# Router logits computed inside the output projection loop, expert ranks from two products, first gathers ahead of the eleventh expert's weights

## The chip, the cores and the metric

The kernel runs on one core of one Trainium2 chip. The metric is the device time of one execution in microseconds (us), as the median of several runs. Beside it stands one profiled execution, from which every duration here is taken. PE is the matrix engine; DVE, ACT and POOL are the vector, scalar and GpSimd engines, SP the engine that issues most DMAs.

## What is computed

One inference step of a decoder layer for 512 prompt rows and 8 sample rows of width 1024: a mixer (a recurrent half and a windowed attention half), cross attention to 256 memory rows, and a mixture of experts. The change touches only the way from the cross attention's output projection into the experts:

```python
x = x + memory_cross_attention(rms_norm(x, lp['norm_cross']), mem_k, mem_v, lp)   # ends in o @ lp['w_co']
x = x + hierarchical_moe(rms_norm(x, lp['norm_ffn']), lp)

def hierarchical_moe(h, lp):
    lg = (hf @ lp['w_group_router'] + lp['b_group_router']).astype(F32)      # 4 groups
    gsel = jnp.argmax(lg, axis=-1)
    p_sel = jnp.sum(jax.nn.softmax(lg, axis=-1) * onehot_g, axis=-1)
    le = (hf @ lp['w_expert_router'] + lp['b_expert_router']).astype(F32)    # 4 groups x 8 experts
    top_v, top_i = lax.top_k(le_sel, TOP_K)                                  # two experts of the chosen group
    top_w = jax.nn.softmax(top_v, axis=-1)
    ...
    # each expert: silu(h @ w_gate) * (h @ w_up) * weight, then @ w_down; summed over the row's two experts
```

## The kernel before, in words

The program is written engine by engine, each engine's instructions in a fixed order, joined by semaphores. Rows are held in five tiles: four of 128 prompt rows (t = 0 to 3) and one of the 8 sample rows (t = 4, `TILES`). PE writes into eight PSUM banks in the order of one list (`bank_plan`, L111): the n-th entry uses bank n mod 8, and PE waits until the entry eight places earlier has been emptied by DVE ("v") or ACT ("a").

The cross attention ends in the loop over `WC_ORDER` = csT, 0, cpT, 1, co, 2, coT, 3, 4. The numbers are the output projections of the row tiles (`cross_output`, L1411, PE); the names are the sample rows' attention: scores transposed (csT), weights transposed (cpT), values (co), outputs transposed (coT). After the projection of tile t, PE transposes the normalised rows of tile t − 1 (`xT3`). On DVE, `residual` (L2122) adds the two halves of the projection to x, empties and scales the transposed rows of the tile before (`gained`, L2145), waits for ACT's sum of squares and its root, and scales the row (L2143); ACT then writes the normalised rows to DRAM (`hn_d`), from where they are gathered later.

After the loop the routing follows, all of it in one chain between PE and DVE:

- PE multiplies all five tiles by the router weights, 36 columns (4 groups and 32 experts), eight products of depth 128 a tile. A float32 product appears as two instructions in the trace.
- DVE adds the bias (L2205), finds the group (`first_max`, L2211), sends the group exponents to ACT and waits for them (L2222 to L2225), masks the other groups, finds the two best experts, and writes a 0/1 table `Mk` of 32 experts for each tile (L2238).
- PE turns the table into ranks, that is, how many rows before this one chose the same expert: for each tile one product with a matrix of ones that goes to all later tiles and the total, and one with a triangular matrix (the loop before `slots`). Meanwhile DVE computes the weights of the two experts (L2240 to L2244).
- DVE turns ranks into slots in blocks of 64 rows (L2246 to L2274) and builds two tables for the ten columns (five tiles, two choices): which block and which row in it (L2275 to L2279). PE multiplies these and so gets for each slot the number of its row. While PE does so, DVE computes which expert an overflow block belongs to (L2281 to L2286, signal `s_eid`).
- DVE makes row indices of it (L2289 to L2297, signal `s_idx`), POOL starts three gathers of 128 normalised rows each (two blocks of 64, L824), and PE starts the 32 expert blocks: transposes (L1473), gate and up products (L1487), down products (L1501).

Expert weights, three loads of 512 KB per expert, go through eleven places in SBUF (`load_expert`, L705). SP issues the first ten while the cross attention and the routing run, each where the place comes free; the tenth waits until the router products have been emptied (its place holds the router weights), the eleventh for `s_idx` (its place holds the routing tables). From the twelfth on each waits for the down products of the block whose place it takes. The router weights themselves (four small loads, L695 to L699) are issued behind the last loads of the cross attention; only PE waits for them, before its router products.

## Time and profile before

| | us |
|---|---|
| median of 3 runs | 850.98 |
| lowest and highest run | 844.87, 852.36 |
| the profiled execution | 848.17 |
| its span, first to last instruction | 846.0 |
| PE busy in the span | 707.3 (84%) |
| DVE busy | 368.9 (44%) |
| mean granted clock of PE | 0.889 of full speed |

The profile comes from one execution. A busy time says how long an engine worked, not that the end waited for it; that is told by the chain, which goes back from the last instruction through whatever released each step. Loads on PE's weight side (PEld) run beside its products. The granted clock is a share of full speed: 1.00 is 2.4 GHz, 0.50 is 1.2 GHz.

### The profile page before, as it was taken

The numbers are of one execution on the slowest core, as the hardware profiler recorded it, in microseconds if no ns is written. First come the engines' busy times: TensorE is split into PE (matmuls) and PEld (weight loads), VectorE is DVE, ScalarE is ACT, GpSimd is POOL, SyncE is SP. The second block draws the span as 40 slices with busy tenths as digits, with TensorE's granted clock in tenths as the row PEclk, the third lists the DMA queues.
The fourth block names the chain that finished last, engine by engine and source line by source line (L and its number), as shares of the span: only waits on it lengthen the run. The fifth ranks groups of instructions, "written<-read, shape, count | busy, mean of one in ns | idle before, by whom it ended". The sixth has DMA issues, their size and how long they took to land.

```text
span 846.0 us, 16080 instructions
## 1 busy us (share of the span) xinstructions
PE 707.3 (84%) x6972; PEld 537.5 (64%) x6972; DVE 368.9 (44%) x717; ACT 214.9 (25%) x538; POOL 92.3 (11%) x122
## 2 busy tenths in 40 slices
PE   4999999999879889567979989858798249999943
PEld 3874887878878878556844458645347247777721
DVE  4210139992365674645682230463143632222217
ACT  4250114334222212434501011331121002222214
POOL 0100000000864000000000000000000013443210
PEclk9999999999999999859989989975896559999966
DMA  9622240002101000410507020032539448999826
GB/s 316 232 100 99 100 148 1 1 1 58 60 3 54 4 3 4 138 22 2 206 1 298 1 100 0 26 100 74 182 125 398 175 143 330 408 405 406 332 78 250
DMA packets 42491, 113.89 MB, mean 135 GB/s; under 512 B 10187, under 2 KB 12677, under 8 KB 41116
## 3 DMA queue, kind: packets, MB, share of 16 engines
q1 hardware_dynamic: 36964, 102.18, 32.7%
q0 software_dynamic: 4864, 8.53, 2.8%
q10 hardware_dynamic: 592, 2.13, 0.7%
q8 instruction: 56, 0.92, 0.4%
q14 instruction: 15, 0.12, 0.0%
HBM read 105.88 MB, written 16.24 MB: 144 GB/s over the span
## 4 chain that ended last, share of the span: by engine, by line
PE 72%; DVE 17%; ACT 4%; issue 3%; DMA 3%; SPq 0%; POOLq 0%; DVEq 0%
PE bank L868 52%; PE bank L1487 7%; PE bank L872 5%; PE bank L1501 4%; PE bank L1473 3%; DVE arena L1911 1%; PE bank L1495 1%; DMA arena<-in_norm_mix 1%; DMA arena<-pair_d 1%; DVE arena L2093 1%; DMA arena<-hn_d,arena 1%; DVE arena L2025 1%; DVE arena L2344 1%; DVE arena L2172 1%; ACT arena L1731 1%
## 5 line engine op out<-in xcount | busy, mean ns | idle before, releaser
L868 PE MATMUL bank<-arena 64*64 64x64 f32 (+12 forms) x5172 | 532.1, 297 | 61.8 <-DMA arena<-pair_d 11.4
L868 PEld LDWEIGHTS bank<-arena 64*64 64x64 f32 (+5 forms) x5172 | 399.0, 160 | 183.6 <-issue 94.2
L872 PE MATMUL bank<-arena 128*128 128x128 f32 (+4 forms) x392 | 57.5, 299 | 52.3 <-issue 16.7
L872 PEld LDWEIGHTS bank<-arena 128*128 128x128 f32 (+4 forms) x392 | 49.9, 166 | 67.5 <-issue 27.5
L1487 PEld LDWEIGHTS bank<-arena 128*64 128x64 f32 x1024 | 58.6, 138 | 19.8 <-issue 19.8
L824 POOL DMA_INDIRECT arena<-hn_d,arena x16 | 16.7, 1044 | 443.9 <-DVE arena L2297 420.1
L1487 PE MATMUL bank<-arena 128*64 128x128 f32 x1024 | 63.5, 277 | 0.0
L2304 DVE TENSOR_TENSOR arena<-bank,arena 128x512 f32<-128x512 f32 x32 | 22.1, 692 | 59.4 <-PE bank L1473 59.4
L1592 ACT COPY arena<-bank 128x260 f32<-128x260 f32 x40 | 15.0, 375 | 108.7 <-PE bank L868 108.7
L828 POOL DMA_INDIRECT pair_d<-arena x32 | 31.8, 993 | 61.1 <-ACT arena L1794 54.1
L2135 DVE TENSOR_TENSOR arena<-arena,bank 128x512 f32<-128x512 f32 x16 | 11.0, 687 | 61.4 <-PE bank L868 61.4
L1692 ACT COPY arena<-bank 128x256 f32<-128x256 f32 x56 | 20.8, 372 | 65.5 <-PE bank L868 64.4
L1501 PE MATMUL bank<-arena 128*64 128x512 f32 x128 | 35.4, 632 | 0.9 <-ACT arena L1790 0.9
L1731 ACT ACTIVATE arena<-arena 128x1024 f32<-128x1024 f32 (+1 forms) x10 | 10.6, 1057 | 97.4 <-DVE arena L2135 90.6
L1867 DVE COPY arena<-arena 128x9 f32<-128x9 f32 x14 | 2.4, 172 | 68.1 <-ACT arena L1592 67.9
L1473 PE MATMUL bank<-arena 128*128 128x128 f32 x128 | 23.4, 312 | 9.4 <-DMA arena<-hn_d,arena 9.4
L1794 ACT COPY arena<-bank 128x512 f32<-128x512 f32 x32 | 18.7, 585 | 46.2 <-PE bank L1501 46.2
L781 POOL TENSOR_TENSOR arena<-arena 128x256 f32<-128x256 f32 x8 | 5.0, 621 | 184.7 <-PE bank L868 184.7
L1473 PEld LDWEIGHTS bank<-arena 128*128 128x128 f32 x128 | 17.6, 197 | 11.5 <-issue 9.5
L2315 DVE TENSOR_TENSOR arena<-arena,bank 128x64 f32<-128x64 f32 x32 | 7.1, 221 | 40.6 <-ACT arena L1788 40.6
L2047 DVE TENSOR_TENSOR arena<-arena,bank 128x256 f32<-128x256 f32 x40 | 16.3, 420 | 12.3 <-PE bank L868 11.7
L2162 DVE TENSOR_REDUCE arena<-bank 128x2 f32<-128x512 f32 x8 | 5.5, 689 | 33.9 <-PE bank L868 33.8
(235 smaller groups left out, 545.8 us busy)
## 6 DMA issues: line engine op xcount, KB each, us to landing
arena<-in_w_exp_gate SPq DMA_DIRECT2D x32, 512.0 KB, 11.8
arena<-in_w_exp_up SPq DMA_DIRECT2D x32, 512.0 KB, 15.0
arena<-in_w_exp_down SPq DMA_DIRECT2D x32, 512.0 KB, 15.7
arena<-in_w_in SPq DMA_DIRECT2D x5, 2048.0 KB, 9.4
arena<-in_x_prompt SPq DMA_DIRECT2D x8, 512.0 KB, 6.1
arena<-in_w_out SPq DMA_DIRECT2D x2, 2048.0 KB, 11.0
arena<-in_cache_mem_k SPq DMA_DIRECT2D x8, 512.0 KB, 7.2
arena<-in_cache_mem_v SPq DMA_DIRECT2D x8, 512.0 KB, 3.8
```

The costliest lines, as they stand in the source:

```text
L824: pool.indirect_dma_start(dst, None, hn_d, bass.IndirectOffsetOnAxis(rows.bitcast(U32), 0), bounds_check=NT - 1, oob_is_err=False).then_in ...
L828: pool.indirect_dma_start(half_rows, bass.IndirectOffsetOnAxis(rows.bitcast(U32), 0), src, None, bounds_check=2 * PAIRS_E - 1, oob_is_err= ...
L868: last[0] = pe.matmul(out, lhsT, rhs, start=start, stop=stop, skip_group_check=True)
L872: last[0] = pe.transpose(out, in_, ident[0:n, 0:n])
L1473: ins = pe.transpose(bX[(2 * p + i) % 3][:, k * P:(k + 1) * P], xk[:, 4 * i + k, :], ident)
L1487: ins = pe.matmul(o[BS * g:BS * g + BS, 0:2 * BS].rearrange("p (a f) -> p a f", a=2), rows[:, k, :], w[:, 0:2, lo:lo + BS], start=k == 0, ...
L1501: ins = pe.matmul(bY[b % 2][BS * n:BS * n + BS, :], actT, wdn[b % NW][:, n * 512:(n + 1) * 512], start=True, stop=True, skip_group_check=True)
L1692: act.copy(dst[(n + 1) % 2][:, 4 * q:4 * q + 4, :], o[:, 0:256].rearrange("p (h t) -> p h t", h=4)).then_inc(evac["a"], 1)
L1731: link(act.activation(junk[0:R, :], x[0:R, t, :], ACT.Square, accum_out=ms))
L1794: act.copy(yb[b % NB3], bY[b % 2][:, :]).then_inc(s_ay, 1)
L2047: tt(Xi[:, qs, :], Xi[:, qs, :], o[:, 0:256].rearrange("p (h t) -> p h t", h=4), ALU.add) \
L2304: tt(xTe[p % 2][:, 4 * i:4 * i + 4, :], bX[n % 3][:, :].rearrange("p (k n) -> p k n", k=4), g, ALU.mult) \
```

## The change

Router products move into the projection loop: after the transposes of tile t − 1 in step t, PE multiplies tile t − 2 by the router weights, so tiles 0, 1 and 2 are done in the loop and tiles 3 and 4 behind it. DVE empties each behind the `residual` of the step. For this the logits get a place that is free earlier, which is zeroed before the loop, behind a new wait for the router weights; the group exponents get a tile of their own (`Tg`). The sums and reciprocals of the group softmax and the experts' weights move behind the row indices. The ranks come from two products over all tiles at once, for which DVE first writes running sums of the table over tiles (`Sc`, one copy and four adds). The tables for the slots are built column by column, in twenty small operations with per-row scalars, and PE multiplies each column as it comes. The overflow experts' numbers move behind the row indices too. On SP, the eleventh expert's weights wait for the third gather to land and for `s_eid` in place of `s_idx`.

```diff
@@ bank_plan
             if step >= 1:
                 g += [(("xT3", step - 1, i), "v") for i in range(2)]
+            if step >= 2:
+                g += [(("route", step - 2), "v")]
     g += [(("xT3", TILES, i), "v") for i in range(2)]
-    g += [(("route", t), "v") for t in range(TILES + 1)]
+    g += [(("route", t), "v") for t in (TILES - 1, TILES)]
...
@@ SP
             done(sp, ("route", 4))
             load_expert(9, 9, s_wgu[9], s_wd[9])
-            sp.wait_ge(s_idx, 1)
+            sp.wait_ge(s_gx[NXG - 1], 16)
+            sp.wait_ge(s_eid, 1)
             load_expert(10, 10, s_wgu[10], s_wd[10])
...
@@ PE, cross_output
                 if t >= 1:
                     rows_transposed("xT3", 5, t - 1)
+                if t >= 2:
+                    route_logits(t - 2)
+
+            def route_logits(t):
+                R = tile_rows(t)
+                if t == 0:
+                    pe.wait_ge(s_rw, 16 * 4)
+                done(pe, ("xT3", t, 1))
+                o = reuse(pe, ("route", t))
+                for k in range(KD):
+                    mm(o[0:R, 0:36], hA[:, k, t * P:t * P + R], wr[:, k, :], k == 0, k == KD - 1)
+                close()
...
             rows_transposed("xT3", 5, TILES)
-            done(pe, ("xT3", 4, 1))
-            pe.wait_ge(s_rw, 16 * 4)
-            for t in range(T5):
...
+            route_logits(TILES - 1)
+            route_logits(TILES)
 
             pe.wait_ge(s_mk, 1)
             o = reuse(pe, ("ranks",))
-            for t in range(T5):
-                later = T5 - t
-                mm(o[:, (t + 1) * NE:(T5 + 1) * NE].rearrange("p (u e) -> p u e", u=later), onesm,
-                   Mk[:, t, :].unsqueeze(1).to_broadcast([P, later, NE]), t == 0, t == T5 - 1)
-                mm(o[:, t * NE:(t + 1) * NE], tri, Mk[:, t, :], False, True)
+            mm(o[:, 0:6 * NE], onesm, Sc.rearrange("p t e -> p (t e)"), True, False)
+            mm(o[:, 0:T5 * NE], tri, Mk.rearrange("p t e -> p (t e)"), False, True)
             close()
 
-            pe.wait_ge(s_slot, 1)
             o = reuse(pe, ("slots",))
             for j in range(J):
+                pe.wait_ge(s_slot, j + 1)
                 for g in range(2):
...
@@ DVE
+            def route_evicted(t):
+                R = tile_rows(t)
+                o = filled(dve, ("route", t))
+                tt(Lg[0:R, t, :], o[0:R, 0:36], rbias[0:R, :], ALU.add).then_inc(evac["v"], 1)
+
+            dve.wait_ge(s_rw, 16 * 4)
+            link(dve.memset(Lg, 0.0))
             for step in WC_ORDER:
...
                     residual("wc", 5, 3, "xT3", step)
+                    if step >= 2:
+                        route_evicted(step - 2)
+            dve.memset(onesm, 1.0)
+            dve.memset(Sc[:, 0, :], 0.0)
+            link(dve.memset(zer, 1.0))
             gained("xT3", TILES, 3)
...
+            route_evicted(TILES - 1)
+            route_evicted(TILES)
...
-            tt(Ta[:, :, 0:4], lg, wide(gmx, 4), ALU.subtract).then_inc(s_exp1, 1)
-            dve.wait_ge(s_exp2, 1)
-            link(dve.tensor_reduce(psel, Ta[:, :, 0:4], X, ALU.add))
-            link(dve.reciprocal(psel, psel))
+            tt(Tg, lg, wide(gmx, 4), ALU.subtract).then_inc(s_exp1, 1)
...
-            tt(Mk, oh[0], oh[1], ALU.add).then_inc(s_mk, 1)
...
+            link(tt(Mk, oh[0], oh[1], ALU.add))
+            link(dve.tensor_copy(Sc[:, 1, :], Mk[:, 0, :]))
+            for t in range(1, T5 - 1):
+                link(tt(Sc[:, t + 1, :], Sc[:, t, :], Mk[:, t, :], ALU.add))
+            tt(Sc[:, T5, :], Sc[:, T5 - 1, :], Mk[:, T5 - 1, :], ALU.add).then_inc(s_mk, 1)
...
-            tt(in_block, iota[:, 0:NBLK].unsqueeze(1).to_broadcast([P, J, NBLK]),
-               slot_block.unsqueeze(2).to_broadcast([P, J, NBLK]), ALU.is_equal)
...
-            tt(in_row, in_row, pair_no1.unsqueeze(2).to_broadcast([P, J, BS]), ALU.mult).then_inc(s_slot, 1)
+            for j in range(J):
+                ts(in_block[:, j, :], iota[:, 0:NBLK], slot_block[:, j:j + 1], None, ALU.is_equal)
+                ts(in_row[:, j, :], iota[:, 0:BS], slot[:, j:j + 1], pair_no1[:, j:j + 1], ALU.is_equal, ALU.mult) \
+                    .then_inc(s_slot, 1)
...
             dve.tensor_copy(halfI, pid).then_inc(s_idx, 1)
+
+            dve.wait_ge(s_exp2, 2)
+            link(dve.tensor_reduce(psel, Tg, X, ALU.add))
...
+            dve.tensor_copy(eidI, eid).then_inc(s_eid, 1)
```

The order of the instructions shows it at three places (line numbers are those of each program; L868 and L872 of before are L874 and L878 of after, product and transpose). First PE, from the transposes behind the projection of tile 2 (`128x128`) to the last router product (36 columns), before:

```order
L872 MATMUL bank<-arena 128x128 x16
L868 MATMUL bank<-arena 128x512 x8
L872 MATMUL bank<-arena 128x128 x8
L868 MATMUL bank<-arena 8x256 x16
L872 MATMUL bank<-arena 128x128 x8
L872 MATMUL bank<-arena 128x8 x8
L868 MATMUL bank<-arena 128x36 x32
L868 MATMUL bank<-arena 8x36 x8
```

and after:

```order
L878 MATMUL bank<-arena 128x128 x8
L874 MATMUL bank<-arena 128x36 x8
L878 MATMUL bank<-arena 128x128 x8
L874 MATMUL bank<-arena 128x512 x8
L878 MATMUL bank<-arena 128x128 x8
L874 MATMUL bank<-arena 128x36 x8
L874 MATMUL bank<-arena 8x256 x16
L878 MATMUL bank<-arena 128x128 x8
L874 MATMUL bank<-arena 128x36 x8
L878 MATMUL bank<-arena 128x8 x8
L874 MATMUL bank<-arena 128x36 x8
L874 MATMUL bank<-arena 8x36 x8
```

The products of tile 0 now stand between the transposes of tile 1 and those of the sample outputs, those of tile 1 ahead of the projection of the sample rows (`8x256`), those of tile 2 ahead of the transposes of the sample rows (`128x8`).

Second DVE, from the slots to the eviction of the slot products (`bank` on the right), before:

```order
L2274 SCALAR_TENSOR_TENSOR arena<-arena 128x10
L2275 TENSOR_TENSOR arena<-arena 128x480
L2277 TENSOR_TENSOR arena<-arena 128x640
L2279 TENSOR_TENSOR arena<-arena 128x640
L2281 TENSOR_TENSOR arena<-arena 128x512
L2283 TENSOR_REDUCE arena<-arena 128x16
L2284 TENSOR_SCALAR arena<-arena 128x16
L2285 COPY arena<-arena 128x1
L2286 CAST arena<-arena 128x17
L2289 TENSOR_SCALAR arena<-bank 128x48
```

and after, with nine of the ten pairs of small operations left out, and from the row indices (`L2299`) on what now follows them:

```order
L2283 SCALAR_TENSOR_TENSOR arena<-arena 128x10
L2285 TENSOR_SCALAR arena<-arena 128x48
L2286 TENSOR_SCALAR arena<-arena 128x64
...
L2291 TENSOR_SCALAR arena<-bank 128x48
...
L2299 CAST arena<-arena 128x48
L2302 TENSOR_REDUCE arena<-arena 128x5
...
L2308 TENSOR_TENSOR arena<-arena 128x512
L2310 TENSOR_REDUCE arena<-arena 128x16
...
L2313 CAST arena<-arena 128x17
L2320 TENSOR_TENSOR arena<-bank,arena 128x512 x3
```

The three wide operations have become ten pairs of small ones, and the expert numbers (512 and 16 columns) stand behind the row indices and ahead of the eviction of the first gathered rows (`L2320`).

Third SP, from the tenth to the twelfth expert's weights, with the semaphores each waits for, before:

```order
L707 DMA arena<-in_w_exp_gate 128x1024 [waits emptied_by_vector]
L708 DMA arena<-in_w_exp_up 128x1024
L709 DMA arena<-in_w_exp_down 128x1024
L707 DMA arena<-in_w_exp_gate 128x1024 [waits row_indices_ready]
...
L707 DMA arena<-in_w_exp_gate 128x1024 [waits down_products]
```

and after:

```order
L712 DMA arena<-in_w_exp_gate 128x1024 [waits emptied_by_vector]
L713 DMA arena<-in_w_exp_up 128x1024
L714 DMA arena<-in_w_exp_down 128x1024
L712 DMA arena<-in_w_exp_gate 128x1024 [waits expert_ids_ready,rows_gathered2]
...
L712 DMA arena<-in_w_exp_gate 128x1024 [waits down_products]
```

The eleventh expert's loads keep their place in the queue and wait for a later signal.

## Rows read from the trace of the kernel before

**Rows 1.** The chain that ended last, in order of time: start us, us, what.

```profile
626.09 6.88 PE bank L868 x16
...
640.31 1.05 PE bank L872 x8
...
641.64 14.95 PE bank L868 x80
...
664.79 4.60 PE bank L868 x20
...
678.22 2.40 PE bank L868 x40
...
683.31 6.52 DMA arena<-hn_d,arena
```

**Rows 2.** Stretches: length, busy us (instructions) by engine, PE clock, DMA share, GB/s.

```profile
604.00:607.30 3.30, 3.30 (x6) 1.53 (x6) 0.22 (x1) 0.00 (x0) 0.00 (x0) 0.50 0.52 211
607.30:624.30 17.00, 17.00 (x71) 7.32 (x70) 4.18 (x7) 2.62 (x5) 0.00 (x0) 1.00 0.08 31
...
637.40:641.40 4.00, 1.04 (x9) 0.95 (x8) 2.77 (x7) 1.99 (x4) 0.00 (x0) 1.00 1.01 331
641.40:656.60 15.20, 14.93 (x80) 14.67 (x80) 1.37 (x8) 0.73 (x1) 0.00 (x0) 0.50 1.02 411
...
664.50:669.50 5.00, 4.58 (x20) 4.45 (x20) 0.85 (x6) 0.81 (x1) 0.00 (x0) 0.50 0.05 18
...
682.40:689.90 7.50, 0.00 (x0) 0.00 (x0) 0.02 (x1) 0.00 (x0) 3.22 (x3) 0.50 0.86 303
...
700.00:805.00 105.00, 105.00 (x1258) 76.84 (x1258) 25.79 (x57) 26.59 (x86) 40.09 (x40) 1.00 0.97 379
```

**Rows 3.** Timeline of DVE, 655 to 681 us: start, us, line, operation, [idle before].

```profile
655.55 0.20 DVE L2205 TENSOR_TENSOR arena<-bank,arena 128x36 f32<-128x36 f32 x1 [3.22 <-PE bank L868]
656.61 0.18 DVE L2205 TENSOR_TENSOR arena<-bank,arena 8x36 f32<-8x36 f32 x1 [0.86 <-PE bank L868]
...
657.89 0.18 DVE L2222 TENSOR_TENSOR arena<-arena 128x20 f32<-128x20 f32 x1
...
658.80 0.18 DVE L2227 TENSOR_SCALAR arena<-arena 128x20 f32<-128x20 f32 x1
659.01 0.60 DVE L2229 TENSOR_TENSOR arena<-arena 128x32 f32<-128x32 f32 x5
...
671.22 0.19 DVE L2256 TENSOR_TENSOR arena<-arena 128x32 f32<-128x32 f32 x1
671.45 0.19 DVE L2258 SCALAR_TENSOR_TENSOR arena<-arena 128x32 f32<-128x32 f32 x1
...
675.90 0.66 DVE L2275 TENSOR_TENSOR arena<-arena 128x480 f32<-128x480 f32 x1
...
678.08 0.69 DVE L2281 TENSOR_TENSOR arena<-arena 128x512 f32<-128x512 f32 x1
...
680.64 0.21 DVE L2289 TENSOR_SCALAR arena<-bank 128x48 f32<-128x48 f32 x1 [0.55 <-PE bank L868]
```

**Rows 4.** The load of the experts' router bias, the last of the four router loads.

```profile
L699 SPq DMA_DIRECT2D arena<-in_b_expert_router x1: 432/432/432, 593.8 to 593.8; - x1
...
DMA to landing us min/median/max: 3.5/3.5/3.5
```

**Rows 5.** Timeline of DVE, 589 to 600 us: sample scores, then tile 0's second add.

```profile
589.99 0.41 DVE L2181 TENSOR_SCALAR arena<-bank 32x256 f32<-32x256 f32 x1 [0.88 <-PE bank L872]
...
598.76 0.69 DVE L2135 TENSOR_TENSOR arena<-arena,bank 128x512 f32<-128x512 f32 x1 [2.75 <-PE bank L868]
```

**Rows 6.** Timeline of DVE, 811 to 813 us: two operations with a per-row scalar.

```profile
811.55 0.28 DVE L2319 TENSOR_SCALAR arena<-arena 128x128 f32<-128x128 f32 x1
811.75 0.28 DVE L2320 TENSOR_SCALAR arena<-arena 128x128 f32<-128x128 f32 x1
```

**Rows 7.** DMA issues, 692.6 to 698 us: count and us to landing.

```profile
arena<-hn_d,arena POOLq DMA_INDIRECT x1, 4.4
```

More of the change, by code:

```diff
@@ L385, in small_kernel @@
         assert off[0] <= 1088
-        Lg = route_region(T5 * 36).rearrange("p (t n) -> p t n", t=T5)
+        Lg = arena[:, at["saved"]:at["saved"] + T5 * 36].rearrange("p (t n) -> p t n", t=T5)
+        assert at["shiftS"] == at["saved"] + RW * 9 and T5 * 36 <= RW * (9 + NS)
+        Tg = route_region(T5 * 4).rearrange("p (t n) -> p t n", t=T5)
         Le = route_region(T5 * NE).rearrange("p (t n) -> p t n", t=T5)
@@ L392, in small_kernel @@
         RC = route_region(6 * NE)
+        Sc = route_region(6 * NE).rearrange("p (t n) -> p t n", t=6)
         slot_all = route_region(T5 * NE).rearrange("p (t n) -> p t n", t=T5)
@@ L1780, in _ @@
             act.wait_ge(s_exp1, 1)
-            act.activation(Ta[:, :, 0:4], Ta[:, :, 0:4], ACT.Exp).then_inc(s_exp2, 1)
+            act.activation(Tg, Tg, ACT.Exp).then_inc(s_exp2, 1)
             act.wait_ge(s_exp1, 2)
@@ L2196, in _ @@
                     residual("wc", 5, 3, "xT3", step)
-            gained("xT3", TILES, 3)
-            link(dve.memset(Lg, 0.0))
-            dve.memset(onesm, 1.0)
-            link(dve.memset(zer, 1.0))
-            for t in range(T5):
-                R = tile_rows(t)
-                o = filled(dve, ("route", t))
-                tt(Lg[0:R, t, :], o[0:R, 0:36], rbias[0:R, :], ALU.add).then_inc(evac["v"], 1)
+                    if step >= 2:
[3 more added lines that the diff above has]
+            link(dve.memset(zer, 1.0))
+            gained("xT3", TILES, 3)
+            route_evicted(TILES - 1)
+            route_evicted(TILES)
             done(dve, ("route", 4))
@@ L2237, in _ @@
                 link(tt(oh[j], oh[j], wide(valid, NE), ALU.mult))
-            tt(Mk, oh[0], oh[1], ALU.add).then_inc(s_mk, 1)
-            dve.wait_ge(s_exp2, 2)
-            link(ts(m1, ee, 1.0, None, ALU.add))
-            link(dve.reciprocal(m1, m1))
-            link(tt(cw[0], m1, psel, ALU.mult))
-            link(tt(cw[1], cw[0], ee, ALU.mult))
+            link(tt(Mk, oh[0], oh[1], ALU.add))
[3 more added lines that the diff above has]
+            tt(Sc[:, T5, :], Sc[:, T5 - 1, :], Mk[:, T5 - 1, :], ALU.add).then_inc(s_mk, 1)
             o = filled(dve, ("ranks",))
@@ L2274, in _ @@
             link(stt(slot, slot_block, float(-BS), slot, ALU.mult, ALU.add))
-            tt(in_block, iota[:, 0:NBLK].unsqueeze(1).to_broadcast([P, J, NBLK]),
-               slot_block.unsqueeze(2).to_broadcast([P, J, NBLK]), ALU.is_equal)
-            link(tt(in_row, iota[:, 0:BS].unsqueeze(1).to_broadcast([P, J, BS]),
-                    slot.unsqueeze(2).to_broadcast([P, J, BS]), ALU.is_equal))
-            tt(in_row, in_row, pair_no1.unsqueeze(2).to_broadcast([P, J, BS]), ALU.mult).then_inc(s_slot, 1)
-            link(tt(big, cum.unsqueeze(1).to_broadcast([P, OVER, NE]),
-                    iota[:, 0:OVER].unsqueeze(2).to_broadcast([P, OVER, NE]), ALU.is_le))
-            link(dve.tensor_reduce(eid[:, 0:OVER], big, X, ALU.add))
-            link(ts(eid[:, 0:OVER], eid[:, 0:OVER], float(NE - 1), None, ALU.min))
-            link(dve.tensor_copy(eid[:, OVER:OVER + 1], cum[:, NE - 1:NE]))
-            dve.tensor_copy(eidI, eid).then_inc(s_eid, 1)
+            for j in range(J):
+                ts(in_block[:, j, :], iota[:, 0:NBLK], slot_block[:, j:j + 1], None, ALU.is_equal)
+                ts(in_row[:, j, :], iota[:, 0:BS], slot[:, j:j + 1], pair_no1[:, j:j + 1], ALU.is_equal, ALU.mult) \
+                    .then_inc(s_slot, 1)
             o = filled(dve, ("slots",))
@@ L2297, in _ @@
             dve.tensor_copy(halfI, pid).then_inc(s_idx, 1)
+            dve.wait_ge(s_exp2, 2)
+            link(dve.tensor_reduce(psel, Tg, X, ALU.add))
+            link(dve.reciprocal(psel, psel))
+            link(ts(m1, ee, 1.0, None, ALU.add))
+            link(dve.reciprocal(m1, m1))
+            link(tt(cw[0], m1, psel, ALU.mult))
+            link(tt(cw[1], cw[0], ee, ALU.mult))
+            link(tt(big, cum.unsqueeze(1).to_broadcast([P, OVER, NE]),
+                    iota[:, 0:OVER].unsqueeze(2).to_broadcast([P, OVER, NE]), ALU.is_le))
+            link(dve.tensor_reduce(eid[:, 0:OVER], big, X, ALU.add))
+            link(ts(eid[:, 0:OVER], eid[:, 0:OVER], float(NE - 1), None, ALU.min))
+            link(dve.tensor_copy(eid[:, OVER:OVER + 1], cum[:, NE - 1:NE]))
+            dve.tensor_copy(eidI, eid).then_inc(s_eid, 1)
             bX, bG = [banks[0], banks[7], banks[1]], [banks[2], banks[6]]
```

5 lines of the change are left out of this document (removed).

## The prediction, made before the result was known

> **What bounds the kernel now.** I read the granted clock and span first, then the page's chain by engine (PE holds 72% of the span), then the chain in order of time from 640 us on, because the change touches only what lies between the output projection of the cross attention and the first expert block. There the chain is one file with nothing beside it [rows 1]: the transposes of the 8 sample rows (from 640.31), one block of router products (14.95 us), choices on DVE until 664.7, the rank products (4.60), slots on DVE, the slot products (2.40), row indices, and the first gather (6.52), after which the first block's transposes start at 689.97. Every microsecond cut there arrives in the time, provided the stretch behind it follows. It does: from 700 to 805 PE is busy 105.00 of 105.00 us [rows 2], so that loop is PE's and moves as a whole. DMA is at 0.97 there, but its weights come through eleven slots and PE never waits for one.
>
> The stretches [rows 2] show two more things. In the projection loop (607.3 to 624.3) PE is busy 17.00 of 17.00 us at clock 1.00, so what is added there is paid for; from 637.4 to 641.4 it is busy 1.04 of 4.00 us, so that gap can take something free. And the router block ran wholly at clock 0.50 (1.2 GHz): the clock fell after that gap, and the block, although it kept PE busy 14.93 of 15.20 us, did not bring it back.
>
> **The change, part by part.** Durations are of the profiled execution (848.17 us, 2.17 of it outside the 846.0 span).
>
> *Router products into the loop.* The block is 80 instructions in 14.95 us; DVE's last two evictions are 655.55 and 656.61 [rows 3], so the 8-row tile costs 1.06 and a full tile (14.95 − 1.06) / 4 = 3.47 at half clock. At full clock I take half, 1.74. Tiles 0 and 1 fall where PE is saturated at clock 1.00: 2 × 1.74 = 3.5 lost. Tile 2 stands behind the last prompt tile's transposes, in the gap that had 2.96 us idle: free. Tiles 3 and 4 stay behind the sample rows' transposes and cost 3.47 + 1.06 = 4.53, if the clock is again 0.50 there. The block's start also no longer waits for the eviction of those transposes (641.36 to 641.64, 0.28). So 14.95 + 0.28 − 4.53 = 10.7 saved, 3.5 lost. The added DVE waits for these products (three evictions in the loop) cost nothing: behind them in DVE's queue stand the sample outputs' copies and the next tile's adds, and PE reaches the products before DVE has finished normalising the same tile. The evictions are 0.2 each.
>
> *The wait for the router weights.* DVE now waits for all four router loads before it touches the sample scores. The last of them is issued at 593.8 and lands 3.5 later, at 597.3 [rows 4]; DVE had begun at 589.99 [rows 5]. Behind that wait stand the memset, three operations on the scores (the first 0.41; 1.0 with the gaps) and the two adds of tile 0 (0.69 each). 597.3 + 0.3 + 1.0 + two adds at 0.6 to 0.7 gives 599.9 in place of 599.45, where the second add ended in the trace after waiting 2.75 us for PE. Its squares and the sample weights' transposes follow in the chain. Cost 0.5. It could be 0 or, if the load lands 1 us later, 1.5.
>
> *Group softmax and weights off the path.* Between L2222's start at 657.89 and L2227 at 658.80 [rows 3] lay the wait for ACT, a reduce and a reciprocal; now L2227's twin follows about 0.1 behind. Saved 0.8. The four weight operations were hidden under the rank products and are worth nothing.
>
> *Running sums added.* One copy and four adds of 128x32, each chained: L2256 and L2258 start 0.23 apart [rows 3], so 5 × 0.22 = 1.1 lost, in front of the rank products.
>
> *Ranks in two products.* 20 instructions took 4.60 [rows 1], 0.23 each. Now 4, with 192 and 160 columns. By count four cost 0.9; by columns, 352 in place of 640, 2.5. The router products, with 36 columns, cost 3.47 / 16 = 0.22 each at the same clock, so columns hardly count at these widths: I take 1.3, near the count. Saved 3.3; the bounds are 2.1 and 3.7.
>
> *Slots by columns.* Three wide operations from 675.90 to 678.16, then 40 products until 680.64, where the eviction starts [rows 3]: 4.74 us. Now 20 small tensor-scalar operations, and PE starts a column as soon as it is built. What does one cost? Two such operations of 128 columns with a pointer scalar start 0.20 apart though each lasts 0.28 [rows 6]; five of 32 columns fill 0.60, so they start 0.10 apart [rows 3]. Between these, 48 columns give 0.12 and 64 give 0.13: ten pairs 2.5 us, 0.1 until the last has ended, 0.25 for PE's last column (2.40 / 10), 0.1 of waits: 2.95. Saved 1.8. The upper bound of the cost is 20 × 0.28 + 0.3 = 5.9, a loss of 1.2. I take the overlapped value; its rows are the same kind of instruction. The Trainium skill speaks against it: "VectorE: DVE Perf Modes", section "The DRAIN you can't avoid", says that the next operation does not start before the pipe of the last has emptied, and to keep the count of operations low. By it the 5.9 would hold; the starts 0.20 apart at 0.28 each speak against it here.
>
> *Expert ids behind the row indices.* They were hidden under the slot products (from 678.08 on). Now six small operations (0.22 apart) and five on ids, two of them of 512 columns (0.69), run after the indices are out: about 3.3 us. The first thing behind them in DVE's queue is the eviction of the first gathered rows, some 6 us later: hidden.
>
> *Gathers ahead of the eleventh expert's weights.* Before, these 1.5 MB were issued at the same signal as the gathers; DMA was 0.86 busy over the wait [rows 2] and the first gather needed 6.52 us from its POOL start [rows 1]. The fourth gather, alone on the engines, took 4.4 [rows 7]. Saved 2.1; the bounds are 0 and 2.3. The load itself is needed some 37 us later (ten blocks at 105 / 28). Behind it in SP's queue stand loads that wait for down products anyway.
>
> **The sum.** 10.7 − 3.5 − 0.5 + 0.8 − 1.1 + 3.3 + 1.8 + 2.1 = 13.6. From the profiled 848.17 that is 834.6; from the shown median 850.98 (runs 844.87 to 852.36) 837.4. The profile stands inside the runs' spread, so I put the forecast between: 836.0.
>
> **The rivals.**
> - *The last two tiles at full clock.* If the third tile's products in the gap keep the clock at 1.00 a little longer, tiles 3 and 4 cost 2.3 instead of 4.5: 833.7. For it: the gap shrinks. Against: the router block itself did not bring the clock back in 15 us [rows 2].
> - *Slower: the clock falls inside the loop.* The 36-column products stand between 512-column ones. If they drop the clock at tile 0 (about 625) and it stays at 0.50, the loop's remaining PE work doubles: the last prompt tile's projection adds 6.9 [rows 1], the work from there (632.97) to the gap at 637.4 up to 4.4, the products of tiles 0 and 1 another 3.5. That is about 15, and 13.6 of gain becomes a loss of 1.4: 851. It decides from some 27 us at half clock on. Against it: at 604.0 to 607.3 the clock was 0.50 under the same wide products and 1.00 from 607.3 on [rows 2]. One short fall costs 1.7.
> - *The small operations don't overlap.* By the page's rule above the slot term is −1.2 for +1.8: 839.0.
> - *The gathers wait for DVE.* POOL now issues them while DVE does eleven operations on SBUF operands; before, DVE stood still. If POOL can't start until DVE is done, 3.3 us behind the indices instead of 0.9, the first gather lands 2.4 later: 838.4. The Trainium skill, "SBUF — State Buffer", section "SBUF: two separate sides", describes such a lock (a GpSimd DMA's descriptors can't be written while DVE runs certain operations). No row here shows the two together.
> - *The gathers are not alone.* The expert loads sent ahead keep DMA at 1.02 during the router block and have ended by about 664.5 (0.05 from there [rows 2]). They are issued 1 to 4 us later now, while the indices come 11.5 earlier, near 671. With 2 to 5 us of margin gone the 2.1 is lost: 838.1.
>
> **How the numbers follow.** Forecast 0.57, full clock at the end 0.15, clock falling in the loop 0.05, no overlap 0.10, DVE's lock 0.08, gathers not alone 0.05. With the two router terms and the wait as one (6.7, from 5.7 to 9.4), the lowest sum of the terms that I hold likely is 5.7 + 0.7 − 1.2 + 3.0 − 1.2 + 0 = 7.0 (from 851 that is 844), the highest 9.4 + 0.9 − 1.0 + 3.4 + 2.0 + 2.3 = 17.0 (from 845 that is 828). So 828 to 844. One per cent, 8.5 us, is about what a measurement of this kernel can tell from no change. All cases but the fall of the clock lie above it; with the spread of the runs I give faster 0.88, same 0.09, slower 0.03.
>
> **What would show it.** In the changed profile: router products of tiles 0 and 1 at clock 1.00 and some 1.7 us each; the sample rows' transposes about 4 us later; the last router eviction near 650; the rank products under 1.5 us; the slot eviction about 3 us after the first small operation; the first gather 4.4 us after its POOL start; the loop's 105 us unchanged. Wrong it would be if the clock row shows 0.50 between 625 and 640, if the small operations start 0.28 apart, or if PE waits for weights in the loop.

## The result, and the profile after

| | before | after |
|---|---|---|
| median of the runs, us | 851.67 (4 runs) | 837.66 (4 runs: 832.23 to 845.13) |
| ratio after / before, 95% interval | | 0.9848 [0.9802, 0.9893] |
| profiled execution, us; its span | 848.17; 846.0 | 839.23; 837.4 |
| mean granted clock of PE | 0.889 | 0.894 |

The change saves 1.5%, some 13 us; the interval ends at 0.9893, just beyond the one per cent that the prediction took as the least that can be told. The forecast was 836.0, with a range of 828 to 844. (One of the four runs, 845.13 us at a mean clock of 0.884, lies over 1.5% above the fastest and is left out of the ratio.)

The chain that ended last, of the changed kernel: start us, us, what. It answers to [rows 1].

```profile
604.85 0.42 PE bank L878 x2
605.27 10.11 PE bank L874 x16
...
627.80 1.71 PE bank L874 x16
...
646.03 1.05 PE bank L878 x8
647.08 4.63 PE bank L874 x32
...
660.21 1.55 PE bank L874 x4
...
668.83 3.78 PE bank L874 x40
...
676.83 5.29 DMA arena<-hn_d,arena
682.16 1.12 PE bank L1480 x4
683.28 5.20 PE bank L1494 x64
```

The block of 14.95 us has become 4.63 for the last two tiles, and 1.71 for each of tiles 0 and 1 in the loop (tile 0's row is shown). The rank products take 1.55 instead of 4.60, but the slot products 3.78 instead of 2.40. Of the gathers, the second one now stands in the chain, not the first. And one row is longer that the change does not touch: the projection of tile 1, 10.11 us at 605.27, was 8.65 at 604.15.

Stretches of the changed kernel: length, busy us (instructions) of PE, PEld, DVE, ACT and POOL, PE clock, DMA share, GB/s. They answer to [rows 2].

```profile
604.50:611.30 6.80, 6.45 (x9) 2.81 (x10) 0.52 (x2) 0.00 (x0) 0.00 (x0) 0.50 0.32 128
...
625.00:642.00 17.00, 17.00 (x112) 11.04 (x111) 7.29 (x22) 2.89 (x6) 0.00 (x0) 1.00 0.65 246
...
646.00:651.60 5.60, 5.57 (x40) 5.38 (x40) 0.88 (x7) 1.28 (x1) 0.00 (x0) 0.50 1.03 418
...
668.20:672.70 4.50, 3.76 (x40) 2.98 (x40) 3.93 (x21) 0.00 (x0) 0.00 (x0) 0.50 0.00 1
674.40:679.90 5.50, 0.00 (x0) 0.03 (x1) 3.06 (x12) 0.00 (x0) 3.21 (x3) 0.50 0.40 102
...
690.40:795.40 105.00, 105.00 (x1258) 76.83 (x1258) 25.78 (x57) 26.59 (x86) 40.10 (x40) 1.00 0.97 379
```

The second row is the loop with the router products in it: PE saturated, clock 1.00, so they did not bring the clock down. The first is where tile 1's projection grew: 0.50 held here for 6.8 us, where before it was 3.3. The last two tiles again ran at 0.50. The last row is the expert loop, 105.00 of 105.00 us as before, only earlier. During the slots (the fourth row) DMA is still: the expert loads are through. The fifth shows POOL's gathers and DVE's eleven moved operations at the same time.

The timeline of DVE and POOL in the changed kernel: start, us, line, operation, out<-in, [idle before <- what ended it]. It answers to [rows 3].

```profile
598.05 0.21 DVE L2191 MEMSET arena<- 128x180 f32 x1 [8.32 <-DMA arena<-in_b_expert_router]
...
651.73 0.18 DVE L2188 TENSOR_TENSOR arena<-bank,arena 8x36 f32<-8x36 f32 x1 [0.86 <-PE bank L874]
...
653.01 0.18 DVE L2235 TENSOR_TENSOR arena<-arena 128x20 f32<-128x20 f32 x1
...
653.31 0.60 DVE L2239 TENSOR_TENSOR arena<-arena 128x32 f32<-128x32 f32 x5
...
658.70 0.33 DVE L2248 TENSOR_TENSOR arena<-arena 128x160 f32<-128x160 f32 x1
...
661.79 0.36 DVE L2255 COPY arena<-bank 128x192 f32<-128x192 f32 x1 [1.63 <-PE bank L874]
...
668.21 0.25 DVE L2285 TENSOR_SCALAR arena<-arena 128x48 f32<-128x48 f32 x1
668.37 0.31 DVE L2286 TENSOR_SCALAR arena<-arena 128x64 f32<-128x64 f32 x1
668.60 0.24 DVE L2285 TENSOR_SCALAR arena<-arena 128x48 f32<-128x48 f32 x1
...
672.63 0.21 DVE L2291 TENSOR_SCALAR arena<-bank 128x48 f32<-128x48 f32 x1 [0.56 <-PE bank L874]
...
674.22 0.19 DVE L2299 CAST arena<-arena 128x48 int32<-128x48 f32 x1
...
675.30 1.22 POOL L830 DMA_INDIRECT arena<-hn_d,arena  x1 [412.07 <-DVE arena L2299]
...
676.83 1.00 POOL L830 DMA_INDIRECT arena<-hn_d,arena  x1 [0.31 <-issue]
...
677.41 0.40 DVE L2313 CAST arena<-arena 128x17 int32<-128x17 f32 x1
```

Read the starts, not the lengths. A small operation with one pointer scalar (48 columns) starts 0.16 us before the next, one with two (64 columns, and a signal) 0.22 to 0.23: a pair takes 0.38. Ten pairs and PE's last column make 4.42 us from 668.21 to the eviction at 672.63. Before it was 4.74.

PE's own timeline of the changed kernel at three places, with its idle time in front: the transposes ahead of tile 1's projection, the products of tile 2 and what follows them, and the transposes that wait for the second gather.

```profile
604.85 0.42 PE L878 MATMUL bank<-arena 32*128 32x32 f32 x2 [5.50 <-DVE arena L1981]
...
642.67 1.87 PE L874 MATMUL bank<-arena 128*128 128x36 f32 x16
646.03 1.05 PE L878 MATMUL bank<-arena 8*128 8x8 f32 x8 [1.49 <-DVE arena L2150]
...
679.90 1.94 PE L1480 MATMUL bank<-arena 128*128 128x128 f32 x8 [7.32 <-DMA arena<-hn_d,arena]
682.16 1.12 PE L1480 MATMUL bank<-arena 128*128 128x128 f32 x4 [0.31 <-DMA arena<-hn_d,arena]
```

### The profile page after: what moved, and what is told of

Read it like the earlier page. It is cut to its first block, busy times and chain, and to the rows that moved or that the text cites. A ratio compares the mean times of both kernels' runs of the same rounds, so it can differ in the third digit from the quotient of the medians.

```text
span 837.4 us, 16076 instructions
## 1 busy us (share of the span) xinstructions
PE 702.7 (84%) x6956; PEld 530.7 (63%) x6956; DVE 371.4 (44%) x740; ACT 214.9 (26%) x538; POOL 92.4 (11%) x122
## 3 DMA queue, kind: packets, MB, share of 16 engines
q0 software_dynamic: 4864, 8.53, 2.9%
## 4 chain that ended last, share of the span: by engine, by line
PE 70%; DVE 18%; ACT 5%; issue 4%; DMA 2%; SPq 0%; POOL 0%; POOLq 0%; DVEq 0%; ACTq 0%
PE bank L874 51%; PE bank L1494 7%; PE bank L878 5%; PE bank L1508 4%; PE bank L1480 2%; DVE arena L1918 1%; PE bank L1502 1%; ACT arena L1667 1%; DMA arena<-pair_d 1%; DVE arena L2100 1%; DVE arena L1963 1%; DVE arena L2032 1%; ACT arena L1684 1%; DVE arena L1990 1%; DMA arena<-hn_d,arena 1%
## 5 line engine op out<-in xcount | busy, mean ns | idle before, releaser
L874 PE MATMUL bank<-arena 64*64 64x64 f32 (+11 forms) x5156 | 527.4, 296 | 60.2 <-DMA arena<-pair_d 11.8
L874 PEld LDWEIGHTS bank<-arena 64*64 64x64 f32 (+5 forms) x5156 | 392.4, 158 | 183.9 <-issue 102.7
L878 PE MATMUL bank<-arena 128*128 128x128 f32 (+4 forms) x392 | 58.2, 301 | 50.9 <-issue 16.6
L878 PEld LDWEIGHTS bank<-arena 128*128 128x128 f32 (+4 forms) x392 | 50.3, 167 | 66.1 <-issue 27.9
L2320 DVE TENSOR_TENSOR arena<-bank,arena 128x512 f32<-128x512 f32 x32 | 22.1, 692 | 54.5 <-PE bank L1480 54.5
```

The source lines that it names most:

```text
L874: last[0] = pe.matmul(out, lhsT, rhs, start=start, stop=stop, skip_group_check=True)
L878: last[0] = pe.transpose(out, in_, ident[0:n, 0:n])
L2320: tt(xTe[p % 2][:, 4 * i:4 * i + 4, :], bX[n % 3][:, :].rearrange("p (k n) -> p k n", k=4), g, ALU.mult) \
```

## The experiments

All are edits of the changed kernel; the ratios are to runs of the kernel before. Line numbers in their rows are their own. Since the clock differs from run to run, two stretches are read beside the times: **S** from the sample scores' transposes (csT) to the first gate/up product, in PE's timeline, and **T1**, the projection of tile 1 inside it, which no edit touches and which differs all the same. The last column is PE's idle time ahead of the sample weights' transposes (cpT), which stand right in front of T1.

| kernel | median us | ratio to before [95%] | S | T1 | idle |
|---|---|---|---|---|---|
| before | | | 103.42 | 8.72 | 5.06 |
| after, first profile | 837.66 | 0.9848 [0.9802, 0.9893] | 93.22 | 10.18 | 5.50 |
| after, again | 838.29 | 0.9871 [0.9839, 0.9903] | 91.12 | 8.53 | 5.40 |
| after, third time | 836.72 | 0.9855 [0.9807, 0.9902] | 90.79 | 8.61 | 5.23 |
| router products behind the loop | 845.49 | 0.9958 [0.9934, 0.9983] | 99.71 | 10.03 | 5.66 |
| ranks in ten products | 839.94 | 0.9886 [0.9847, 0.9924] | 95.01 | 10.17 | 5.51 |
| slots in three wide operations | 833.82 | 0.9809 [0.9781, 0.9837] | 91.50 | 9.88 | 5.88 |
| the same, again | 837.08 | 0.9851 [0.9816, 0.9885] | 91.40 | 8.51 | 5.43 |
| block table wide, row table small | 836.70 | 0.9852 [0.9819, 0.9884] | 90.00 | 8.51 | 5.44 |
| router weights waited for late | 836.35 | 0.9848 [0.9820, 0.9877] | 90.39 | 8.73 | 5.06 |
| eleventh load earlier | 838.69 | 0.9889 [0.9851, 0.9927] | 91.28 | 9.97 | 5.77 |
| gathers as before, slots wide | 838.62 | 0.9882 [0.9834, 0.9929] | 95.92 | 10.19 | 5.48 |
| tile 3's router products early | 835.06 | 0.9823 [0.9790, 0.9855] | 88.65 | 8.51 | 5.43 |
| three edits together | 832.94 | 0.9800 [0.9759, 0.9842] | 87.84 | 8.72 | 5.06 |

**The changed kernel again.** No edit.

> The changed kernel once more, beside which the next three stand. Ratio to the kernel before 0.980 to 0.990. The marker stretch from the transposes of the routing rows (589.99 us in the first profile) to the first gate/up product (683.28) is again 93.3, within 0.5, where the half clock falls at the same places; if the 1.46 us by which tile 1's projection grew was chance, it is 8.65 here, if it belongs to the change it is 10.1 again.

S is 91.12, 2.1 below the first profile; 1.65 of that is T1, which is back at 8.53. So T1's growth came and went with the run. The third profile has 8.61.

**The router products put back.**

```diff
-                if t >= 2:
-                    route_logits(t - 2)
...
-            route_logits(TILES - 1)
-            route_logits(TILES)
+            for t in range(T5):
+                route_logits(t)
```

> All five tiles' router products go back behind the loop, ten accumulated groups of them at the half clock of that stretch; the other parts of the change stay. Forecast of the prediction's own term: the time rises by 7.2 us (10.7 saved at the end less 3.5 in the loop), ratio to before about 0.993. Rival, that the products cost in the loop what they save behind it (they break the run of the projection's products): no rise, ratio 0.985. In the trace the products of five tiles take some 11.5 us in one piece after the sample rows' transposes, at clock 0.50, and the loop of projections is 3.4 us shorter.

PE's timeline of this kernel:

```profile
609.18 10.03 PE L872 MATMUL bank<-arena 128*128 128x512 f32 x16
...
647.68 14.93 PE L872 MATMUL bank<-arena 128*128 128x36 f32 x80
```

The block is 14.93 us long again (I had written 11.5, which was wrong arithmetic: five tiles at half clock are 14.9). S rises by 8.59, of which 1.50 is T1: 7.1, beside the 7.2 of the prediction. By the ratios it is (0.9958 − 0.9871) × 849 = 7.4. The rival, no rise, falls. T1 is long here although no router product stands in the loop, so these products are not its cause.

**The ranks put back.**

```diff
-            mm(o[:, 0:6 * NE], onesm, Sc.rearrange("p t e -> p (t e)"), True, False)
-            mm(o[:, 0:T5 * NE], tri, Mk.rearrange("p t e -> p (t e)"), False, True)
+            for t in range(T5):
+                later = T5 - t
+                mm(o[:, (t + 1) * NE:(T5 + 1) * NE].rearrange("p (u e) -> p u e", u=later), onesm, ...)
+                mm(o[:, t * NE:(t + 1) * NE], tri, Mk[:, t, :], False, True)
```

> The ranks go back to ten products and the running sums go; the rest of the change stays. By the prediction's terms the time rises by 2.2 us (3.3 for the products less 1.1 for the sums); by the first trace of the changed kernel by 2.0 (3.11 less 1.12). Rival, that a later wait takes up what the ranks save (the gathers wait for something else): no rise. In the trace PE starts the ranks 0.39 us after the mask and needs 4.6.

The mask's last operation, PE's products and DVE's copy behind them, in this kernel's timeline:

```profile
660.34 0.33 DVE L2251 TENSOR_TENSOR arena<-arena 128x160 f32<-128x160 f32 x1
...
660.72 4.58 PE L874 MATMUL bank<-arena 128*128 128x160 f32 x20 [7.39 <-DVE arena L2251]
...
665.34 0.36 DVE L2254 COPY arena<-bank 128x192 f32<-128x192 f32 x1 [4.67 <-PE bank L874]
```

From the start of the mask's last operation (660.34) to the copy it is 5.00 us, with two products and the sums 3.09 (658.70 to 661.79 in the first profile of the changed kernel). So sums and products together are worth 1.9. S rises by 3.89, 1.64 of it T1. The times, 0.0015 apart with intervals of 0.004, could not have told it.

**The slots put back, twice.**

```diff
-            for j in range(J):
-                ts(in_block[:, j, :], iota[:, 0:NBLK], slot_block[:, j:j + 1], None, ALU.is_equal)
-                ts(in_row[:, j, :], iota[:, 0:BS], slot[:, j:j + 1], pair_no1[:, j:j + 1], ALU.is_equal, ALU.mult) \
-                    .then_inc(s_slot, 1)
+            tt(in_block, ..., ALU.is_equal)
+            link(tt(in_row, ..., ALU.is_equal))
+            tt(in_row, in_row, pair_no1..., ALU.mult).then_inc(s_slot, 1)
```

> The slot tables go back to three wide operations and one signal; the rest stays. The prediction's term was 1.8 us, so the time would rise by 1.8; the first trace of the changed kernel has 4.42 from the first small operation to the end of the slots' eviction where the kernel before had 4.74, so by the trace it rises by 0.3 only. That is read from the stretch in the trace and not from the time, which cannot tell 0.3 from nothing.

> The kernel with the slot tables in three wide operations, once more: the same program as in the fourth run, whose time came out at 0.9809 of the kernel before against 0.9871 for the changed kernel, though in the two profiles the stretch from the first slot operation to the slots' eviction is 4.73 and 4.43 us, the other way, and the two profiles part by 1.9 us already before 590 us, where both run the same code. If the 0.6% belongs to the slot tables, the ratio is 0.981 again, within 0.003; if it is the clock's chance, it comes nearer to 0.987.

DVE's timeline in the second of the two:

```profile
668.66 0.66 DVE L2284 TENSOR_TENSOR arena<-arena 128x480 f32<-128x480 f32 x1
...
673.40 0.21 DVE L2292 TENSOR_SCALAR arena<-bank 128x48 f32<-128x48 f32 x1 [2.48 <-PE bank L874]
```

4.74 us, as before the change, against 4.43 with the small operations (668.17 to 672.60 in the second profile of the changed kernel). The columns are worth 0.3, not 1.8. The times were a trap: the first six runs had a median of 833.82, 4.5 us under the changed kernel beside them, and would have made this edit a gain. The second six of the same program have 837.08. S is 91.50 and 91.40 in the two profiles, so the difference does not come from the slots; the first profile reaches S at 589.78, the second at 592.39, 2.6 us later, in code that is the same.

**The block table alone put back.** Only `in_block` becomes one wide operation again.

> The block table goes back to one wide operation and only the row table keeps ten small ones, each with a signal. If what a small operation costs is its two pointer operands (0.22 us from start to start with two, 0.155 with one), the ten take 2.2 us after 0.57 of the wide one, PE follows a column every 0.24, and the stretch from the first operation to the start of the slots' eviction is 3.5 to 3.7 instead of 4.42. If a small operation costs the same whatever its operands (0.19 each), PE gains the same ten places, 0.57 + 10 x 0.19, and the stretch is 3.3 to 3.5. If PE was the bound with 0.37 per column, it stays above 4.2. The time: 0.7 to 0.9 us less than the changed kernel, which the times cannot tell from nothing.

DVE's timeline of this kernel, from the block table to the slots' eviction:

```profile
666.69 0.66 DVE L2284 TENSOR_TENSOR arena<-arena 128x480 f32<-128x480 f32 x1
667.26 2.32 DVE L2287 TENSOR_SCALAR arena<-arena 128x64 f32<-128x64 f32 x10
...
670.14 0.21 DVE L2292 TENSOR_SCALAR arena<-bank 128x48 f32<-128x48 f32 x1 [0.56 <-PE bank L874]
```

3.45 us in place of 4.42. The total lies inside the range of the second theory and 0.05 under that of the first, but the starts speak for the first: ten operations fill 2.32, the last of them 0.31 long, so they start (2.32 − 0.31) / 9 = 0.22 apart, not 0.19. It is a cost of the form of the operation. Whether the second pointer or the signal makes it 0.22 and not 0.16 was not separated. PE needs about 0.24 for a column, so now both run at nearly one pace.

**The router weights waited for late.**

```diff
-            dve.wait_ge(s_rw, 16 * 4)
-            link(dve.memset(Lg, 0.0))
...
+                    if step == 2:
+                        dve.wait_ge(s_rw, 16 * 4)
+                        link(dve.memset(Lg, 0.0))
```

> DVE's wait for the router weights and the clearing of the logits move from ahead of the sample scores to just ahead of the first router eviction. The prediction priced the wait at 0.5 us and the first trace of the changed kernel has 0.44: the sample scores' operations start right after the bank's products again, and the idle of PE ahead of the sample weights' transposes falls from 5.4 or 5.5 us to 5.0. Time 0.4 to 0.5 us less. Rival, that the later start of tile 1's projection is why it ran 10.2 us at the half clock in three of four profiles: then it is 8.7 here and the time falls by 2.

PE's timeline of this kernel, at the sample weights' transposes:

```profile
604.38 0.36 PE L878 MATMUL bank<-arena 32*128 32x32 f32 x2 [5.06 <-DVE arena L1981]
```

PE's idle is 5.06 us, that of the kernel before; from csT to this row it is 14.42 us, against 14.86, 14.76 and 14.58 in the three profiles of the changed kernel. The wait cost 0.2 to 0.4. T1 is 8.73 here, but it was short with the wait in two of those three as well. Over all profiles T1 was long in 6 of 11 with the wait and in 0 of 3 without. The last column of the table puts them in order: ahead of the six long ones PE had been idle for 5.48 to 5.88 us, ahead of the eight short ones for 5.06 to 5.44, and all three at 5.06 are the kernels without the wait. So the wait, which lengthens this idle time, probably makes a long T1 likelier. No run changed the idle time alone, so this is argued and not shown.

**The eleventh load earlier.**

```diff
-            sp.wait_ge(s_gx[NXG - 1], 16)
             sp.wait_ge(s_eid, 1)
```

> SP's eleventh load of expert weights no longer waits for the third gather, and is issued as soon as the experts' numbers are there (some 677.8 us, after the first two gathers and beside the third); the other parts of the change stay. If what the gathers gain comes from having the DMA engines to themselves, the gathers behind the first land later by what the load's packets take: the stretch from POOL's first gather to the first gate/up product goes from 7.9 us to 9.0 to 11, and the time rises by 1 to 3 us. Rival, that the gain comes only from the first gather, which the load can no longer meet: the stretch stays within 0.3 of 7.9 and the time does not move.

The timelines of POOL (first gather), SP (eleventh load) and PE (first gate/up products) in this kernel, in order of time:

```profile
675.07 1.22 POOL L829 DMA_INDIRECT arena<-hn_d,arena  x1 [413.13 <-DVE arena L2298]
...
677.60 0.33 SPq L712 DMA_DIRECT2D arena<-in_w_exp_gate  x1
...
682.64 4.40 PE L1493 MATMUL bank<-arena 128*64 128x128 f32 x64
```

675.07 to 682.64 is 7.57 us; the changed kernel has 7.91, 7.73 and 7.60. The first theory falls: a load that starts 2.5 us behind the first gather does no harm up to the first product, and the wait for the third gather could go. Either the load never matters or its place ahead of the gather does. The next run tells.

**The gathers as before.** On top of the three wide slot operations: the load waits for the row indices only, and the eleven operations on weights and experts stand ahead of the indices again.

```diff
-            sp.wait_ge(s_gx[NXG - 1], 16)
-            sp.wait_ge(s_eid, 1)
+            sp.wait_ge(s_idx, 1)
             load_expert(10, 10, s_wgu[10], s_wd[10])
```

> The gathers alone are undone, on top of the three wide slot operations (so that the experts' numbers are hidden under the slot products as in the kernel before): the eleventh load is sent at the row indices' signal again, 0.9 us ahead of the first gather, and the eleven operations on weights and experts stand ahead of the indices. Beside it stands the kernel with the wide slot operations, where POOL's first gather to the first transposes takes 4.7 us and to the first gate/up product 7.7. If what counts is that the load's packets are queued ahead of the gather's, the first becomes 6.5 to 6.7 and the second 9.3 to 9.6, and the time rises by 1.6 to 1.9. If the load sent some 2 us after the first gather (the eighth run) did no harm because the load never does, both stay within 0.3. The eleven operations cost nothing in either case (1.3 us of them in the 1.63 of the rank products, 2.2 in the 2.48 of the slot products).

The same three timelines of this kernel, with PE's first transposes, and ahead of them DVE's last operation on the experts' numbers:

```profile
672.23 0.18 DVE L2301 CAST arena<-arena 128x17 int32<-128x17 f32 x1
...
674.76 0.33 SPq L712 DMA_DIRECT2D arena<-in_w_exp_gate  x1
...
675.62 1.23 POOL L829 DMA_INDIRECT arena<-hn_d,arena  x1 [412.38 <-DVE arena L2312]
...
683.03 2.80 PE L1479 MATMUL bank<-arena 128*128 128x128 f32 x12 [10.13 <-DMA arena<-hn_d,arena]
685.86 0.48 PE L1493 MATMUL bank<-arena 128*64 128x128 f32 x2
```

The load is issued 0.86 us ahead of the gather, and the first transposes come 7.41 us behind the gather's start instead of 4.71, the first gate/up product 10.24 instead of 7.72: 2.5 us. By the ratios it is 0.0031, 2.6 us, from the second run of its neighbour, though their intervals overlap. So it is the load's place ahead of the gather that costs: 0.86 us ahead costs 2.5, 2.5 behind costs nothing. Places between these were not run.

**Tile 3's router products early.** They move ahead of the sample rows' transposes, with their bank.

```diff
+            route_logits(TILES - 1)
             rows_transposed("xT3", 5, TILES)
-            route_logits(TILES - 1)
             route_logits(TILES)
```

> The router products of the last prompt tile move ahead of the sample rows' transposes, into the gap where PE waits 1.49 us for DVE. From the start of tile 2's products (642.67 in the first trace) to the last router eviction (651.91) it is 9.24 us with the changed kernel. If tile 3's products take 1.87 there at clock 1.00 as tile 2's do, and the sample rows' transposes start 0.4 later, the stretch is 9.24 - 3.5 + 0.4 = 6.1 to 6.5, and the time falls by 2.7 to 3.1. If they wait for DVE's scaling of tile 3 as long as the transposes wait now, or the clock falls under them as well, the stretch is 7.5 to 9.2, and the time falls by 0 to 1.7.

The timelines of PE (router products of tiles 2 and 3) and DVE (the last router eviction) in this kernel:

```profile
643.03 1.87 PE L875 MATMUL bank<-arena 128*128 128x36 f32 x16
645.24 1.98 PE L875 MATMUL bank<-arena 128*128 128x36 f32 x16 [0.33 <-DVE arena L2158]
...
649.64 0.18 DVE L2189 TENSOR_TENSOR arena<-bank,arena 8x36 f32<-8x36 f32 x1 [1.22 <-PE bank L875]
```

Tile 3's products take 1.98 (the clock is 1.00 from 643.0 to 647.2), and from 643.03 to the end of the last eviction it is 6.79 us instead of 9.24. That lies between the two theories, since the sample rows' transposes start 0.8 later rather than 0.4. 2.4 us are saved; the time falls by 1.7 between neighbours.

**Three edits together.** The late wait, the wide block table and tile 3's early products.

> Three edits at once on the changed kernel: the wait for the router weights moved to the first router eviction, the block table by one wide operation, tile 3's router products in the gap. Their terms add up: 0.45 + 0.95 by the traces of the runs with the first two alone, and 0 to 3 for the third: 1.4 to 4.4 us below the changed kernel beside it, ratio to before 0.980 to 0.984 where that has 0.985 to 0.987. If the clock's chance swamps it, the stretches show it all the same: from the sample scores' transposes to the first gate/up product 2 to 4 us less at the same clock.

> The changed kernel a third time, as the neighbour of the three runs before it: ratio to before 0.983 to 0.988. In the trace the slots take 4.42 us from the first small operation to the eviction, and POOL's first gather to the first gate/up product 7.9.

S is 87.84, 2.95 below its neighbour's 90.79, with T1 about equal. The three terms (0.3 + 1.0 + 2.4) would give 3.7; of the rest, 0.30 is the stretch from the first gather to the first gate/up product, 7.90 us here and 7.60 in the neighbour. The median is 3.8 us lower, but the intervals of the two ratios overlap a little, so the size is the stretches' to tell. With 0.9800 [0.9759, 0.9842] of the kernel before it is the fastest version found, though its lead on tile 3's early products alone (0.9823) is not clear of the noise; the 0.9809 of the wide slots did not repeat.

## Why the prediction was right, and where not

| step | forecast | first profile | the run that undoes it |
|---|---|---|---|
| router products | 10.7 − 3.5 | 15.23 − 4.63 − 2 × 1.71 = 7.2 | 7.1 |
| wait for the router weights | −0.5 | −0.4 | −0.2 to −0.4 |
| group softmax off the path | 0.8 | 0.8 | not undone |
| sums and ranks | −1.1 + 3.3 | −1.1 + 3.1 | 1.9 |
| slots by columns | 1.8 | 0.3 | 0.3 |
| gathers ahead | 2.1 | 1.6 | 2.5 |
| clock in tile 1 | – | −1.5 | long in 6 of 11 with the wait, 0 of 3 without |
| sum | 13.6 | 10.0 | |

S fell by 10.2 in the first pair of profiles, and by 12.3 and 12.6 in the other two of the changed kernel, in which tile 1 was not slowed; the ratio gives 12.9. So the forecast stood on the right terms, though that the median came within 1.7 us of it is partly luck, as two medians of one program lie 3.3 apart here (833.82 and 837.08). Over half of it rests on one term: the router block, which ran at 0.50 behind a gap in PE's work and now runs at 1.00 for three of five tiles. The group softmax is the one term that rests on the two profiles alone: from the subtraction ahead of the exponents to the masking it was 657.89 to 659.01, and is 653.01 to 653.31. Halving the 3.47 for the full clock gave 1.74; it measured 1.71. That tile 2 is free in the gap held too (its products take 1.87 from 642.67, and PE then still waits 1.49 for DVE ahead of the transposes at 646.03), and the last two tiles, forecast at 4.53, took 4.63.

*The step that failed* is "Slots by columns". The prediction took the start distance of a small operation from five without a pointer scalar (0.10) and two with one (0.20 at 128 columns), interpolated by columns alone and wrote 0.12 and 0.13. The runs have 0.16 with one pointer and 0.22 with two and a signal: 0.38 for a pair, ten pairs 3.8 instead of 2.5. DVE, not PE, then sets the pace of the products (3.78 instead of 2.40). The bounds, −1.2 to 2.0, held it, and this miss of 1.5 is most of what lies between the 13.6 and the 12.3 to 12.6 by which S fell without a slow tile 1. The Trainium skill, "VectorE: DVE Perf Modes", section "The DRAIN you can't avoid", says that the next operation does not start until the pipe of the last is empty, and also that one which is not held starts earlier. The first half alone, as the prediction read it, gives starts as far apart as the operations last (5.9 us in all); the trace has operations of 0.25 and 0.31 starting 0.16 and 0.23 apart, so they overlap.

*The wait for the router weights* itself cost 0.2 to 0.4, near the 0.5 forecast. What the sum had no term for is the clock behind it: in the first profile PE's idle time there was 5.50 us instead of 5.06, and tile 1 stayed at 0.50 for longer and took 1.5 more. Whether the wait is the cause stays open.

*The gathers.* First gather to transposes fell from 6.66 to 4.60, as forecast. What the prediction left out is that PE's third set of transposes, in front of the gate and up products, waits for the second gather (0.31 idle at 682.16), so only 9.48 − 7.91 = 1.6 arrived; in the third profile, where PE does not wait for it, 9.48 − 7.60 = 1.9 did. The reason given, the engines to themselves, was half right: the load may run beside the gathers, only not queued ahead of them.

*The rivals.* The clock did not fall in the loop. DVE did not hold up POOL: its three gathers last 1.22, 1.00 and 0.99 beside DVE's eleven operations (3.06 us in the stretch shown) and 1.23, 1.00 and 0.99 with DVE idle in the run with the gathers as before, and the first starts 1.08 behind the start of the last index operation in both (674.22 to 675.30 in the changed kernel). So the lock that the prediction took from the Trainium skill, "SBUF — State Buffer", section "SBUF: two separate sides", in which DVE holds up POOL, does not show with these operations. One operation of DVE may be held up by POOL instead: the last of the eleven, of 17 columns at 677.41, takes 0.40 and ends with the second gather (677.81 and 677.83). It takes 0.39 or 0.40 in all twelve profiles in which the two run together, and 0.18 with POOL idle in the run with the gathers as before. It costs no time here, since DVE's next work comes at 681.03; why it is so was not tested. The gathers were alone: DMA was still from 668.2 to 672.7. The rival at full clock came in part: twice (the first wide slots and the earlier load) the last two tiles took 3.2 us, else 4.3 to 4.7.

## What to carry to other kernels

A serial block behind a gap in an engine's work may pay the half clock for its whole length: put its parts where the engine is already busy, and the rest into the gap itself. When wide operations are split into small ones so that another engine can follow, count the starts of the very form, pointer scalars and signals included, since the split pays only if its rate reaches the follower's. And where two transfers leave at one signal, queue the one first that is waited for.

## What was not expected

The same program gave a median of 833.82 us in one set of six runs and 837.08 in another, with intervals that overlap only a little. For edits of one or two microseconds the stretches of the profile were the measurement, and the times only a check.

Tile 1's projection, untouched by every edit, takes 8.5 to 8.7 us in eight profiles and 9.9 to 10.2 in six, as the clock stays at 0.50 for longer or shorter behind PE's wait of some 5 us. That alone is 0.2% of the time. In the long ones that wait was 5.48 to 5.88 us, in the others 5.06 to 5.44. So a fraction of a microsecond added to a wait in front of PE may cost more behind it than the wait itself; that this is the cause was not shown.
